# S5 table blocks in FFN one: two blocks per visit of TensorE, behind every second pair, with a second pair of PSUM banks

## What is computed

```
h = rms_norm(x, norm2_g[l])
x = x + (jax.nn.silu(h @ w_gate[l]) * (h @ w_up[l])) @ w_down[l]
```

```
bu_re = jnp.einsum('gpc,bkgc->bkgp', bb_re, u_c)
...
y = (jnp.einsum('gcp,bkgp->bkgc', c_re, x_re)
     - jnp.einsum('gcp,bkgp->bkgc', c_im, x_im))
```

## Time and profile before

| | us |
|---|---|
| median of 3 runs | 1019.65 (1019.57 to 1021.81) |
| profiled execution, its time | 1019.17 |
| its span, first to last instruction | 1017.4 |
| TensorE matmul busy | 983.0 (97%) |
| DVE busy | 619.4 (61%) |
| ScalarE busy | 491.2 (48%) |
| POOL busy | 318.3 (31%) |

### The profile page before, as it was taken

One profiled execution on the slowest core, in us unless ns is written; L12 is line 12 of the kernel. 1 busy time (PEld: TensorE's weight loads), 2 busy tenths in 40 slices (PEclk: granted clock), 3 DMA queues, 4 the chain that ended last, 5 costly groups with the idle time before them and its releaser, 6 DMA issues.

```text
span 1017.4 us, 17069 instructions
## 1 busy us (share of the span) xinstructions
PE 983.0 (97%) x6960; PEld 879.0 (86%) x6960; DVE 619.4 (61%) x640; ACT 491.2 (48%) x647; POOL 318.3 (31%) x321
## 2 busy tenths in 40 slices
PE   8999899999999999999999999999989999999997
PEld 6987689999987788787689999988968889999885
DVE  4899676666653545566575655545685575555544
ACT  6765464444433465544464444334456464434332
POOL 5670457887999111199310000000100010000000
PEclk9999899999999999999899999999999999999999
DMA  9741046776667855555256555555954545655541
GB/s 337 258 145 62 1 142 215 228 226 213 225 217 221 258 166 158 156 163 167 85 164 188 184 175 196 168 205 196 412 202 164 175 157 172 200 165 196 175 166 42
DMA packets 130994, 186.79 MB, mean 184 GB/s; under 512 B 4736, under 2 KB 103552, under 8 KB 130432
## 3 DMA queue, kind: packets, MB, share of 16 engines
q1 hardware_dynamic: 106944, 158.54, 47.9%
q10 hardware_dynamic: 24000, 27.54, 7.9%
HBM read 174.54 MB, written 15.73 MB: 187 GB/s over the span
## 4 chain that ended last, share of the span: by engine, by line
PE 84%; DVE 9%; ACT 4%; issue 2%; DMA 1%; ACTq 0%; POOL 0%; DVEq 0%; SPq 0%; POOLq 0%
PE ps L407 14%; PE ps L409 14%; PE ps L408 14%; PE ps L456 7%; PE ps L458 7%; PE ps L460 7%; PE ps L428 4%; PE ps L430 3%; PE ps L429 3%; DVE cacc L2005 2%; ACT whi L361 2%; DVE wlo L367 2%; PE ps L834 1%; PE ps L853 1%; DVE x_res L639 1%
## 5 line engine op out<-in xcount | busy, mean ns | idle before, releaser
L367 DVE TENSOR_TENSOR wlo<-wraw,whi 128x2048 fp32r<-128x2048 f32 x143 | 341.5, 2388 | 239.6 <-ACT whi L361 239.5
L361 ACT ACTIVATE whi<-wraw 128x2048 fp32r<-128x2048 f32 x143 | 273.8, 1915 | 375.7 <-PE ps L409 219.6
L407 PE MATMUL ps<-actH,whi 128*128 128x256 f32 x1232 | 351.4, 285 | 1.1 <-DVE actL L578 1.0
L409 PE MATMUL ps<-actH,wlo 128*128 128x256 f32 x1232 | 348.6, 283 | 0.0
L408 PE MATMUL ps<-actL,whi 128*128 128x256 f32 x1232 | 348.6, 283 | 0.0
L407 PEld LDWEIGHTS ps<-actH,whi 128*128 128x128 f32 x1232 | 236.3, 192 | 4.3 <-issue 3.8
L408 PEld LDWEIGHTS ps<-actL,whi 128*128 128x128 f32 x1232 | 236.4, 192 | 0.1
L409 PEld LDWEIGHTS ps<-actH,wlo 128*128 128x128 f32 x1232 | 236.4, 192 | 0.0
L607 POOL TENSOR_SCALAR rs<-ss 128x1 f32<-128x1 f32 (+2 forms) x16 | 4.0, 252 | 514.3 <-ACT nat L593 444.1
L456 PE MATMUL ps<-whi,gH 128*128 128x512 f32 x264 | 82.0, 392 | 0.0
L458 PE MATMUL ps<-wlo,gH 128*128 128x512 f32 x264 | 81.4, 389 | 0.0
(11 more groups left out here) (355 smaller groups left out, 1346.1 us busy)
## 6 DMA issues: line engine op xcount, KB each, us to landing
wraw<-in_ffn_w_gate SPq DMA_DIRECT2D x22, 1024.0 KB, 5.3
wraw<-in_ffn_w_up SPq DMA_DIRECT2D x22, 1024.0 KB, 5.3
wraw<-in_ffn_w_down SPq DMA_DIRECT2D x22, 1024.0 KB, 4.9
wraw<-in_fox_w_in SPq DMA_DIRECT2D x16, 1024.0 KB, 5.4
wraw<-in_w_gate SPq DMA_DIRECT2D x11, 1024.0 KB, 5.3
wraw<-in_w_up SPq DMA_DIRECT2D x11, 1024.0 KB, 5.6
wraw<-in_w_down SPq DMA_DIRECT2D x11, 1024.0 KB, 5.0
wraw<-in_w_in SPq DMA_DIRECT2D x9, 1024.0 KB, 11.2
```

The costliest lines, as they stand in the source:

```text
L361: act.activation(self.whi[:, n0 % RING, :], self.wraw[:, n0 % RAW, :], ACT.Copy).then_inc(self.hi_done, 1)
L367: dve.tensor_tensor(self.wlo[:, n0 % RING, :], self.wraw[:, n0 % RAW, :], self.whi[:, n0 % RING, :].bitcast(F32), ALU.subtract).then_inc(s ...
L407: pe.matmul(out, wh, self.actH[:, k, :], start=(i == 0), stop=False)
L409: last = pe.matmul(out, wl, self.actH[:, k, :], start=False, stop=(i == KT - 1))
```

## The change

- `over_pairs`: in the loop the two calls of `prep` stand behind both pairs, so blocks 1 and 2 follow pair 2, blocks 3 and 4 follow pair 4, and so on to blocks 9 and 10. This moves TensorE's and ScalarE's part. Block 0 stays.
- Down part, new function `prep_under_down`: blocks 11 and 12 behind unit 3, 13 and 14 behind unit 7, 15 behind unit 9, on both engines.
- New function `prep_banks`: even blocks keep banks 6 and 7; odd blocks use banks 2 and 3 in the up part and 4 and 5 in the down part.
- `pe_prep` now waits for the copies of block b-2, whose banks it takes, where it waited for those of b-1.
- `pe_ffn` waits for `prep_kout` of blocks 0 to 10 ahead of the down part, which accumulates in banks 0 to 3.
- `pool_prep`, the slots `rtb`, `ob`, `rsb` and `ksb`, DVE and SP are unchanged.

```diff
             for j in range(2):
                 one(2 + 2 * j, 1 + j, it, 2)
-                if prep:
-                    prep(1 + j, it, 2)
+            if prep:
+                prep(1, it, 2)
+                prep(2, it, 2)
...
         base = self.ffn_banks(a)[2]
+        if prep:
+            pe.wait_ge(*self.past("prep_kout", FP))
         for i in range(FT // 2):
...
-            if prep and i % 2 == 1:
-                self.pe_prep(pe, a, FP + i // 2)
+            for b in self.prep_under_down(i) if prep else ():
+                self.pe_prep(pe, a, b)
...
-            if prep and i % 2 == 1:
-                self.act_prep(act, a, FP + i // 2)
+            for b in self.prep_under_down(i) if prep else ():
+                self.act_prep(act, a, b)
...
+    def prep_under_down(self, i):
+
+        return {3: (FP, FP + 1), 7: (FP + 2, FP + 3), 9: (FP + 4,)}.get(i, ())
+
+    def prep_banks(self, a, b0):
+
+        if b0 % 2 == 0:
+            return a + 2, a + 3
+        return (a - 2, a - 1) if b0 < FP else (a, a + 1)
+
     def pe_prep(self, pe, a, b0, it=0, step=0):
+        turned, kernel = self.prep_banks(a, b0)
         b = b0 + step * it
         s = b0 % 2
         pe.wait_ge(*self.past("prep_pool", 6 * b + 6))
-        if b0 > 0:
-            pe.wait_ge(*self.past("prep_rout", b))
+        if b0 > 1:
+            pe.wait_ge(*self.past("prep_rout", b - 1))
+            pe.wait_ge(*self.past("prep_kout", b - 1))
+        elif b0 == 1:
             pe.wait_ge(*self.past("prep_kout", b))
...
-            last = pe.transpose(self.ps[:, a + 2, i * P:(i + 1) * P],
+            last = pe.transpose(self.ps[:, turned, i * P:(i + 1) * P],
...
-            last = pe.matmul(self.ps[32 * i:32 * i + 32, a + 3, 0:P],
+            last = pe.matmul(self.ps[32 * i:32 * i + 32, kernel, 0:P],
...
-        act.activation(self.rsb[:, s], self.ps[:, a + 2, :].rearrange("p (i c) -> p i c", i=GB), ACT.Copy)\
+        act.activation(self.rsb[:, s], self.ps[:, turned, :].rearrange("p (i c) -> p i c", i=GB), ACT.Copy)\
...
-        act.activation(self.ksb[:, s, P:2 * P], self.ps[:, a + 3, 0:P], ACT.Copy)\
+        act.activation(self.ksb[:, s, P:2 * P], self.ps[:, kernel, 0:P], ACT.Copy)\
```

## The result

The changed kernel takes 1058.84 us (median of 4 runs, 1058.25 to 1060.08), the kernel before 1020.39 us beside it. The ratio is 1.0377, 95% interval 1.0359 to 1.0395. The profiled execution took 1059.34 us with a span of 1057.6 us, 40.2 us more than the earlier trace rows. I had forecast slower, 1046 us, with a range of 1034 to 1057: the sign and the places of the waits in the up part were right, one term, the lag, was too small, and the time lies 1.8 us above the range.

The account below looks back on a forecast made before the run. TensorE was taken to bound FFN one, with POOL close behind. Waits for POOL 15.0, gate 3.8 and clock 8.4, less joints 0.7, add 26.5 us to 1019.17: 1045.7, stated as 1046 us, range 1034 to 1057.

Parts of the forecast that it names:

- the lag: Time from a visit's start to POOL's refill of a block slot; taken as 8.2 us, 6.9 in the down part.
- B and D: Merged visits of blocks 3, 4 and of 7, 8, up part: TensorE waits 5.2 us for POOL at each.
- A, C and E: Merged visits of blocks 1, 2, of 5, 6 and of 9, 10, up part: no wait for POOL.
- F, G and H: Down-part visits of blocks 11, 12, of 13, 14 and of 15: waits for POOL of 0.4, 4.2 and 0 us.
- The lag is 11.4 us everywhere: Rival, 10%: stores of two blocks crowd each other and the weight loads, so every refill comes late; 1058 us.
- POOL catches up: Rival, 12%: during TensorE's stalls POOL makes blocks in 9.7 us, waits at B and D fall to 2.0 us; 1036 us.
- The gate: Ahead of the down part TensorE waits until ScalarE has copied out blocks 0 to 10: 3.8 us of stall.
- The clock: TensorE's clock falls to half behind four stalls longer than 2.5 us: 2.1 us each, 8.4 us in all.
- The joints: Steps into and out of the small matmuls at seven merged visits: 0.1 us saved each, 0.7 us in all.

Follow-up runs that it names:

- r2_gate10: Changed kernel, with the wait ahead of the down part covering the copies of blocks 0 to 9 only; 1057.24 us, ratio 1.0362.
- r10_warm_again: Changed kernel with FFN one's loops written out and four stalls filled with unread matmuls, the last at blocks 13 and 14; 1051.83 us, ratio 1.0291.
- r9_down_only: Changed kernel with one block behind every pair of the up part again, so only the down part's blocks stay merged; 1029.54 us, ratio 1.0085.

## Why the prediction was too low

- **What bounds, and the cause.** Right: TensorE sets the stage's end, POOL has two slots, and giving both back together makes it late. The third slot took the waits for POOL away (0.2 us left of 24 to 26).
- **The pattern of the waits.** Right in the up part: stalls at B and D, none at A, C and E. In the down part I had put the wait at G; it was spread over F, G and H, and in other runs sat at F or G. Their sum was 9.6 us for my 4.6.
- **The lag.** This is the step that failed. I took 8.2 us, "median 8.2", of seven lags from 7.2 to 11.4, as if each were drawn by chance. They were not: the lag was 10.8 to 11.4 us where the weight load was issued ahead of the last store or within 0.1 us behind it, and 7.2 to 8.2 us where it came 0.2 us behind it or later. With POOL idle DVE's split took 2.29 to 2.30 us at A, C and E, and the load fell within 0.1 us of the store each time: lags of 12.3, 11.8 and 11.6 us. Less the 1.3 us that POOL's first block was faster, that made the waits at B and D 8.0 and 7.7 us for my 5.2, 2.8 and 2.5 us more. At F to H they were 9.6 for 4.6 us, with lags of 11.6, 6.9 and 9.7 us for my 8.2, 6.9 and 6.9; there the clock fall that I had put behind G, and which did not come, also brought TensorE to H 2.1 us sooner, to wait there. Holding the load back gave lags of 7.0 to 8.2 us.
- **The rival that came true.** "The lag is 11.4 us everywhere", to which I gave 10%, comes to 1058 us, and that is the time. Its waits for POOL are 25.5 us, measured 25.3. Some of that is luck: it has 11.4 us behind A, C and E but 6.9 behind F and G, and takes 11.3 us for every block, so that a lag too short and a first block too long cancel. Of its reason, that stores and weight loads crowd each other, the weight load is shown; the stores of two blocks are not needed, and whether they add something is open.
- **POOL catches up.** Half of that rival came true: of two blocks made in a row the first took 10.0 and 10.1 us (B and D), where it had 9.7, but the second 11.4.
- **The gate.** 3.8 us forecast, 3.9 measured. I had counted it, with its clock fall, against POOL's time at F (the 30.5 us), and rightly; as a term of its own the 3.8 us are not what the gate costs, since with less of it the wait at F grows (r2_gate10).
- **The clock.** 8.4 us forecast, 9.3 measured behind the stalls, four falls. One of them was behind H and not behind G. Like the gate's, this term is not a gain to be had: with the stalls filled the total did not fall.
- **The joints.** 0.7 us forecast, 0.2 measured. The rule that I had weighed from the Trainium skill, "TensorE: Matmul & The Clock Gate", section "Architectural detail: the array is 16× 32×32, not 1× 128×128" (weight loads pulled ahead), would make it nothing. The time comes nearer to that than to the 2.6 us of the rows' upper end, but the trace shows another reason: a new joint of 0.20 us in the place of each old one.
- **The range.** It ended at 1057, just below that rival's 1058. 1.8 us of the profiled difference lie ahead of the stage, where the change does nothing and the prediction had nothing.

## What to carry to other kernels

Before two uses of a double buffer are moved together, ask when both buffers come back: the producer that had 25 us for each of two overlapping steps then has 25 us for the lag and both steps in a row. A latency that takes several values in a trace is not to be averaged before it is known what sets it; here the issue time of a transfer on another queue did, and the change itself made that time the same at every double visit. When one stall is taken out of a stage that a slower producer paces, look at the next wait before counting the gain.

## What the runs showed of the hardware

- A store of 256 KB landed 2.5 to 3.3 us behind its issue where a 1 MB load on another queue was issued 0.23 us or more behind it (kernel before, four visits of the table), and 5.8 to 7.3 us where the load was issued 0.5 us ahead of it or up to 0.08 us behind it (three visits before, three after). At 0.3 us it took 2.8 to 8.6 us over all runs.
- A VectorE split that began 0.05 us behind a GpSimd product took 3.26 us instead of 2.29 (209.27); where the split began 0.02 us ahead of the product, it took 2.29 us and the product 3.31 instead of 1.18 (234.28).
- TensorE's granted clock fell from 1.00 (2.4 GHz) to a mean of 0.58 behind B, most of that window at the level of 1.2 GHz, although the matmuls ahead of the idle time were dense. The falls behind B, D, the gate and H (stalls of 8.0, 7.7, 3.9 and 6.8 us) took 1.7 to 2.8 us each from the stretch behind them. The length of the idle time alone did not decide: it fell behind 2.1 us in r10_warm_again (0.72) and stayed at 1.00 behind 2.65 us at the gate of r9_down_only (287 to 291 us). Idle matmuls in the stall kept it at 1.00.
- Issuing a DMA of 8 KB from ScalarE took 3.73 us once, and delayed the weight split behind it, where it took 0.45 us before.
